# A written table of step orders, one-pass cumulative sums and a folded query norm in a two-block transformer kernel

## The chip, the cores and the metric

The kernel runs on one core of a Trainium2 chip. The metric is the device time of one execution in microseconds. A core has five engines that run their own queues in order: TensorE (PE, with its weight loads shown as PEld), VectorE (DVE), ScalarE (ACT), GpSimd (POOL) and SyncE (SP), which here issues all DMAs. They wait for one another through semaphores.

## What is computed

The reference is one layer of two different transformer blocks, over 512 positions of width 1024, in fp32. The parts around the change are the first block's two causal attentions and the second block's delta rule, which is followed by a norm over each head:

```python
def stick_breaking_attention(q, k, v):          # 8 heads of 64
    ...
    log_rem = jnp.where(strict, jax.nn.log_sigmoid(-z), 0.0)
    after = lax.cumsum(log_rem, axis=3, reverse=True) - log_rem
    w = jnp.where(strict, jnp.exp(jax.nn.log_sigmoid(z) + after), 0.0)
...
def _gated_deltanet(q, k, v, alpha, beta, a_log, dt_bias):   # 8 heads of 128, chunks of 64
    q = _l2norm(_to_chunks(q.astype(f32), A_HEADS, A_DK)) * (A_DK ** -0.5)
    k = _l2norm(_to_chunks(k.astype(f32), A_HEADS, A_DK))
    ...
    U = ut - jnp.einsum("bhck,bhkv->bhcv", wt, S)
    o = jnp.einsum("bhck,bhkv->bhcv", qt, S) + jnp.einsum("bhcj,bhjv->bhcv", pt, U)
    ...
oa = rmsnorm_2(oa, head_norm[l]) * jax.nn.silu(za.reshape(b, s, A_HEADS, A_DV))
```

Here `_l2norm(x)` is `x * rsqrt(sum(x * x) + EPS)` and `rmsnorm_2` divides by the root of the mean square plus `EPS`, 1e-6. Beside these there are a forgetting attention (8 heads of 64), a memory attention, gates, a banded attention with bias (16 heads of 64), a cross attention (4 heads of 256) and two feed-forward parts.

## The kernel before

All weight products (`Schedule.gemm`, `product`) multiply a 128x128 weight block with 512 columns of the transposed activations. Both operands are split into a high and a low part in fp32r, and three matmuls replace one (high by high, high by low, low by high: L1065, L1067, L1071). SyncE loads four blocks (`stage`), ScalarE makes their high parts (`whi`, L1520), VectorE or GpSimd the low parts (`wlo`, L1917, L2411). A step `mm` is two blocks, so six matmuls; a gemm over 1024 inputs is four such steps and an eviction step `ev`. Everything else on TensorE is an fp32 matmul through the helper `mm` (L1017) or a transpose (L1020).

`Schedule` builds one list of steps, and each engine goes through this list in the same order and issues what is its own. A part of the kernel is a generator that yields steps; an empty step keeps a distance. `mix` and `pipe` take turns between generators, and `par` spreads several lists evenly over one another by their lengths:

```python
        i = min((i for i in range(len(parts)) if done[i] < len(parts[i])), key=lambda i: (done[i] + 0.5) / len(parts[i]))
        yield parts[i][done[i]]
```

The parts that `par` spreads are, with names used below:
- `sb_pair(p)`, four pairs of stick-breaking heads, beside the weight products of the next pair: scores (`sb_z`), absolute value, exponential and logarithm (`sb_ln`), softplus (`sb_sp`), the cumulative sum on TensorE (`sb_cum`, in five pieces between which VectorE adds later blocks to earlier ones, `sb_after`), weights (`sb_w`), values (`sb_o`).
- `soft_pair("fox", p, ...)` beside products with head norms (`hn_sq`, `hn_mm`, `hn_out`) and `mem_pair(n)`, whose scaled softmax (`mp_n`, tile `sbW`) TensorE transposes.
- for each head h of the delta rule: products of head h+1 with its convolutions, silu and l2 norms (`gdn_proj`), preparation (`gdn_prep`: `gp_kk`, `gp_xy`, then five times `gp_P` and `gp_Y`, `gp_uw`) and the scan of head h-1 (`gdn_scan`: `gc_w` and `gc_s` for eight chunks, called W and S with the chunk's number below, `gc_o`, the output norm, `gs_oz`). A `gc_s` needs VectorE's subtraction into `cuu` after `gc_w`.
- band attention, the memory norm and the cross attention, each beside weight products.

A "spare" bank is the one of the two gemm banks that the running gemm does not use. A norm's ones-product goes there, and the next gemm can open only when ScalarE's logarithm has read it.

Of the kernel before, what the change touches and what calls it, by code (L numbers as in the profile page):

```python
# [8 lines left out]
F32 = mybir.dt.float32  # L9
# [7 lines left out]
T = 512  # L17
# [26 lines left out]

IDLE = 20
# [96 lines left out]
class Kernel:  # L142
# [43 lines left out]
    def allocate(self):  # L186
        sb, two = self.sb, range(2)
        self.x, self.eps = sb("x", [128, 8, T]), sb("eps", [128, 1])
# [27 lines left out]
    def allocate_block1(self):  # L216
# [14 lines left out]
        self.sbA, self.sbW = [sb(f"sbA{i}", [128, 1280]) for i in two], [sb(f"sbW{i}", [128, 1280]) for i in two]  # L231
# [15 lines left out]
    def allocate_block2(self):  # L247
# [5 lines left out]
        self.ce = [sb(f"ce{i}", [128, T]) for i in two]  # L253
# [69 lines left out]
def par(*parts):  # L323
    parts = [list(p) for p in parts]
    done = [0] * len(parts)
    while any(n < len(p) for n, p in zip(done, parts)):
        i = min((i for i in range(len(parts)) if done[i] < len(parts[i])), key=lambda i: (done[i] + 0.5) / len(parts[i]))
        yield parts[i][done[i]]
        done[i] += 1


@dataclass(eq=False)
class Norm:
# [14 lines left out]
    u_out: Use  # L348
    halves: tuple = ()
# [24 lines left out]
class Schedule:  # L374
# [3 lines left out]

# [29 lines left out]
    def halved_norm(self, no, out, u_out, raw, raw_ref, ones, scale, gain):  # L408
# [3 lines left out]
                 Use("sqb1", [("hn_out", no)]), Use("spare", [("hn_ln", no)]), u_out, (k.ofx[0][:, 3, :], k.ofx[1][:, 3, :]))  # L412
# [92 lines left out]
    def sb_pair(self, p):  # L505

        two = []
        for hh in range(2):
# [4 lines left out]
            u["A"], u["W"] = Use(f"sbA{hh}", [("pe_cum", (h, 0))]), Use(f"sbW{hh}", [("pe_o", h)])  # L513
# [128 lines left out]
    def block1(self):  # L642
# [5 lines left out]
        nxt = [mix(self.left, pipe(self.sb_proj(1)), islice(norm, 9)), mix(pipe(self.sb_proj(2) + kv[0]), norm), pipe(self.sb_proj(3) + kv[1]), seq(  # L648
            self.proj("w_in", 3072, k.qr[0][:], Use("qr0", [("pe_small", "fox")]), "mix"),
            mix(self.fox_forget(None), pipe(self.fox_proj(0))))]  # L650
# [5 lines left out]
        yield [st("none", None, *(Use(f"mq{i}", ends[i // 2]) for i in range(4)), *(Use(f"mmp{x}", ends[x]) for x in range(2)),  # L656
                  *(Use(f"{n}{x}", [("pe_cum", (("sb", 3, x), 0))]) for n in ("fxp", "fxpt", "mmpt") for x in range(2)))]
# [64 lines left out]
    def gdn_proj(self, h):  # L722
# [11 lines left out]
        if h == 8:  # L734
            yield [x for s_ in later(7) for x in s_]
            for _ in range(5):
                yield []
# [1923 lines left out]
```

## Time and profile before

| | |
|---|---|
| median of 3 runs | 2276.83 us (2276.15 to 2276.99) |
| profiled execution, its own time | 2276.96 us |
| its span, first to last instruction | 2274.9 us |
| instructions | 34567 |
| TensorE busy | 2238.1 us, 98% |
| VectorE busy | 1192.0 us, 52% |
| ScalarE busy | 932.0 us, 41% |
| GpSimd busy | 424.9 us, 19% |
| granted TensorE clock | 0.999 of full speed |

All of it is from one execution. Matmuls are pipelined and their ends are modelled, so the start of one matmul to the start of the next says more than the busy time. The stages in the trace: start to 28 us, stick-breaking pairs to 190, forgetting and memory pairs to 360, gates and first feed-forward to 930, start of the delta rule to 985, its heads to 1345, gates and band attention to 1790, cross attention to 1870, second feed-forward to the end.

### The profile page before, as it was taken

The numbers are of one execution on the slowest core, as the hardware profiler recorded it, in microseconds if no ns is written. First come the engines' busy times: TensorE is split into PE (matmuls) and PEld (weight loads), VectorE is DVE, ScalarE is ACT, GpSimd is POOL, SyncE is SP. The second block draws the span as 40 slices with busy tenths as digits, with TensorE's granted clock in tenths as the row PEclk, the third lists the DMA queues.
The fourth block names the chain that finished last, engine by engine and source line by source line (L and its number), as shares of the span: only waits on it lengthen the run. The fifth ranks groups of instructions, "written<-read, shape, count | busy, mean of one in ns | idle before, by whom it ended". The sixth has DMA issues, their size and how long they took to land.

```text
span 2274.9 us, 34567 instructions
## 1 busy us (share of the span) xinstructions
PE 2238.1 (98%) x13120; PEld 1796.2 (79%) x13120; DVE 1192.0 (52%) x2236; ACT 932.0 (41%) x1761; POOL 424.9 (19%) x356
## 2 busy tenths in 40 slices
PE   9999999999999999999999999999999999999998
PEld 6776778888888888777777788777788988888887
DVE  5435654445644546565556514665656446535454
ACT  5544554333322323444444332444435534323234
POOL 2332221001201102423343242000011001101001
PEclk9999999999999999999999999999999999999999
DMA  5223212333333333321121124223233413332332
GB/s 176 82 62 96 70 49 77 97 98 98 96 96 96 97 97 93 101 78 52 52 60 59 43 70 129 80 84 84 66 93 108 142 49 102 93 102 93 102 93 93
DMA packets 108643, 199.60 MB, mean 88 GB/s; under 512 B 12208, under 2 KB 14384, under 8 KB 108224
## 3 DMA queue, kind: packets, MB, share of 16 engines
q1 hardware_dynamic: 108480, 197.41, 28.7%
q8 instruction: 105, 1.72, 0.3%
q14 instruction: 58, 0.48, 0.1%
HBM read 195.20 MB, written 2.16 MB: 87 GB/s over the span
## 4 chain that ended last, share of the span: by engine, by line
PE 94%; DVE 3%; ACT 2%; issue 1%; DMA 0%; SPq 0%; POOL 0%; DVEq 0%; ACTq 0%
PE bank L1065 26%; PE bank L1071 25%; PE bank L1067 25%; PE bank L1017 14%; PE bank L1020 3%; DVE ya L1917 0%; DVE sbA L2107 0%; DMA x<-in_xT 0%; DVE fout L1917 0%; DVE sqb L1917 0%; ACT sbA L1661 0%; DVE acc L1917 0%; ACT sqb L1560 0%; DVE cx L1920 0%; ACT hh L1539 0%
## 5 line engine op out<-in xcount | busy, mean ns | idle before, releaser
L1065 PE MATMUL bank<-hh,whi 128*128 128x512 f32 x1680 | 684.2, 407 | 4.8 <-ACT sqb L1560 2.5
L1071 PE MATMUL bank<-hh,wlo 128*128 128x512 f32 x1680 | 656.7, 391 | 1.2 <-POOL wlo L2411 0.6
L1067 PE MATMUL bank<-hl,whi 128*128 128x512 f32 x1680 | 655.2, 390 | 0.3 <-DVE hl L1920 0.3
L1520 ACT ACTIVATE whi<-stage 128x512 fp32r<-128x512 f32 x682 | 425.4, 626 | 551.0 <-PE bank L1071 542.2
L1917 DVE TENSOR_TENSOR wlo<-stage,whi 128x512 fp32r<-128x512 f32 x506 | 408.3, 825 | 88.6 <-ACT whi L1520 84.6
L1065 PEld LDWEIGHTS bank<-hh,whi 128*128 128x128 f32 x1680 | 315.8, 188 | 75.3 <-issue 5.3
L1071 PEld LDWEIGHTS bank<-hh,wlo 128*128 128x128 f32 x1680 | 315.3, 188 | 70.7 <-DVE wlo L1917 1.9
L1067 PEld LDWEIGHTS bank<-hl,whi 128*128 128x128 f32 x1680 | 316.2, 188 | 63.2 <-issue 3.8
L2411 POOL TENSOR_TENSOR wlo<-stage,whi 128x512 fp32r<-128x512 f32 x176 | 234.2, 1336 | 450.9 <-ACT whi L1520 450.8
L1917 DVE TENSOR_TENSOR x<-bank,x 128x512 f32<-128x512 f32 (+1 forms) x81 | 55.5, 685 | 176.0 <-PE bank L1071 175.9
L1065 PE MATMUL bank<-u1h,whi 128*128 128x512 f32 x256 | 99.6, 389 | 0.0
L1067 PE MATMUL bank<-u1l,whi 128*128 128x512 f32 x256 | 99.6, 389 | 0.0
L1071 PE MATMUL bank<-u1h,wlo 128*128 128x512 f32 x256 | 99.6, 389 | 0.0
L2411 POOL TENSOR_TENSOR acc<-acc,sqb 128x512 f32<-128x512 f32 x34 | 45.7, 1345 | 283.1 <-ACT sqb L1533 283.1
L2411 POOL TENSOR_TENSOR u1l<-f1t,u1h 128x512 fp32r<-128x512 f32 x32 | 41.3, 1292 | 264.4 <-ACT u1h L1632 264.4
L2411 POOL TENSOR_TENSOR u2l<-f2s,u2h 128x512 fp32r<-128x512 f32 x22 | 28.4, 1290 | 299.0 <-ACT u2h L1641 299.0
L1017 PEld LDWEIGHTS bank<-ya 64*64 64x64 f32 (+1 forms) x2048 | 58.5, 137 | 25.0 <-issue 14.7
L1017 PE MATMUL bank<-ya 64*64 64x64 f32 (+2 forms) x2048 | 72.0, 231 | 1.9 <-DVE ya L1917 1.9
L1065 PE MATMUL bank<-u2h,whi 128*128 128x512 f32 (+1 forms) x182 | 69.7, 383 | 0.0
L1067 PE MATMUL bank<-u2l,whi 128*128 128x512 f32 (+1 forms) x182 | 69.6, 383 | 0.0
L1071 PE MATMUL bank<-u2h,wlo 128*128 128x512 f32 (+1 forms) x182 | 69.5, 382 | 0.0
L1632 ACT ACTIVATE u1h<-f1t 128x512 fp32r<-128x512 f32 x32 | 20.3, 634 | 111.4 <-DVE f1t L1917 111.4
(377 smaller groups left out, 3376.1 us busy)
## 6 DMA issues: line engine op xcount, KB each, us to landing
stage<-in_wall SPq DMA_DIRECT2D x682, 256.0 KB, 2.7
band<-in_toep SPq DMA_DIRECT2D x16, 256.0 KB, 3.5
x<-in_xT SPq DMA_DIRECT2D x8, 256.0 KB, 6.0
fb<-rowsf SPq DMA_DIRECT2D x8, 256.0 KB, 3.9
gbc<-rows SPq DMA_DIRECT2D x8, 256.0 KB, 3.3
gbc<-rowsc SPq DMA_DIRECT2D x16, 128.0 KB, 3.6
out_y<-fout SPq DMA_DIRECT2D x8, 256.0 KB, 2.5
memx<-in_memT SPq DMA_DIRECT2D x1, 1024.0 KB, 9.5
```

What stands on the lines that cost most here:

```text
L1017: return pe.matmul(out, w, r, start=start, stop=stop, skip_group_check=True)
L1020: return pe.transpose(out, in_, k.cf("ident"))
L1065: pe.matmul(o, wh, hi, start=j == 0, stop=False)
L1067: pe.matmul(o, wh, lo, start=False, stop=False)
L1071: i = pe.matmul(o, wl, hi, start=False, stop=end)
L1520: act.activation(k.whi[u % NSPLIT][:], k.stage[u % NSTAGE][:], ACT.Copy).then_inc(*up("whi", u))
L1632: act.activation(k.u1[0][:, a["t"] % 16, :], a["b"][:], ACT.Copy).then_inc(*up("sp_hi", ("u1", a["t"])))
L1917: return dve.tensor_tensor(out, a, b, op)
L2411: return pool.tensor_tensor(out, a, b, op)
```

## The change

Three things change together.

`par` and the empty steps go. `paced(key, work, *chains)` takes the same steps without the empty ones, as strands: letter a is all weight products in a row, the next letters are the tails of products that have one (turn or head norm), and the last letters are the chains (pair, preparation, scan). It yields them in the order that the string `ORDERS[key]` spells. There are 26 strings.

The cumulative sum of a stick-breaking head is made in one go. ScalarE copies the softplus tile into fp32r (`sb_high`, into the space of `ofx`), VectorE subtracts to get the low part (`sb_low`, in the space of `sbW`), and TensorE adds all blocks with two fp32r passes of ten matmuls each. The constants `ntri` and `nones` are copied once into fp32r (`cfr`). The five pieces and VectorE's additions between them go.

The query of the delta rule is no longer normalized. ScalarE squares it with a factor (`query_square`), GpSimd adds that to the square of the output (`scan_sum`), and the output norm uses another epsilon (`eps2`), so that the norm of the output makes up for the query's. `gp_qd` and the query-key product wait for the silu instead of the norm. The third buffer set `gq2` takes the place of `ce`.

```diff
+ORDERS = {
+    "sb0": "eadeaadadaeadaeadaedaaedcaaedaedab",
+    "sb1": "haggaagaagaaaghaagaaahggagaahaaaabcaaacahahdcaaadadahaaaeaheeafff",
...
+    "sb3": "aafaafabafabafaaafcaacfcaaadaafafdaed",
...
+    "fox0": "gaagagaaabgaagbabgaacgaacgagcaagdaadgadgaaegaaeagaefg",
...
+    "fox3": "bacacabcacbaacacbbcaabaccabacabcacaabccbaacabacbacacbcabcabac",
...
+    "head0": "caaacacabcababbabacacabbbbbbaaccacbacbbabbcaacabacb",
...
+    "head": "acdcacdcaadabbbbcbadaacdcdacacabbbbcdabcdacbdbcabcadcbacbdacbacdabcadbc",
...
+    "band": "caaccacaacacacacaacacbcacacacac",
...
+    "cross3": "bcabcacbabcbcbcabccbacba",
+}
...
-        self.sbA, self.sbW = [sb(f"sbA{i}", [128, 1280]) for i in two], [sb(f"sbW{i}", [128, 1280]) for i in two]
+        self.sbA = [sb(f"sbA{i}", [128, 1280]) for i in two]
+        self.cfr = sb("cfr", [128, 256], F32R)
+        m4 = len(self.open)
+        self.sbl = [sb(f"sbl{i}", [128, 1280], F32R) for i in two]
+        self.close(m4)
+        self.sbW = [sb(f"sbW{i}", [128, 1280]) for i in two]
+        self.sbh = [flat(o)[:, 0:1280] for o in self.ofx]
...
-def par(*parts):
-    parts = [list(p) for p in parts]
-    done = [0] * len(parts)
-    while any(n < len(p) for n, p in zip(done, parts)):
-        i = min((i for i in range(len(parts)) if done[i] < len(parts[i])), key=lambda i: (done[i] + 0.5) / len(parts[i]))
-        yield parts[i][done[i]]
-        done[i] += 1
-
...
+    def paced(self, key, work, *chains):
+
+        strands, tails, needs = [[]], {}, {}
+        for n, (g, tail, *need) in enumerate(work):
+            for x in need:
+                needs.setdefault(x, len(strands[0]))
+            strands[0] += [s for s in g if s]
+            if tail:
+                tails[len(strands)] = n
+                strands.append([s for s in tail if s])
+        strands += [[s for s in c if s] for c in chains]
+        order = ORDERS[key]
+        left = [iter([s for s in c if s[0][0] not in ("need", "mark")]) for c in strands]
+        for c in order:
+            yield next(left[ord(c) - 97])
+        assert not any(next(c, None) for c in left), key
...
-            u["A"], u["W"] = Use(f"sbA{hh}", [("pe_cum", (h, 0))]), Use(f"sbW{hh}", [("pe_o", h)])
+            u["A"], u["W"] = Use(f"sbA{hh}", [("sb_hi", h), ("sb_lo", h)]), Use(f"sbW{hh}", [("pe_o", h)])
+            u["H"], u["L"] = Use(f"sbh{hh}", [("pe_cum", h)]), Use(f"sbW{hh}", [("pe_cum", h)])
             two.append(Head(h, "sb", p, hh, u, "osb"))
         yield [st("sb_z", two, *(o.uses[b] for o in two for b in range(3)))]
         yield [st("sb_ln", o, o.uses["A"]) for o in two]
         yield []
         yield []
-        yield [st("sb_sp", o) for o in two]
-        a, b = two
-        yield [st("sb_cum", (a, 3))]
-        for s in (2, 1, 0):
-            yield [st("sb_cum", (a, s)), st("sb_cum", (b, s + 1))]
-        yield [st("sb_cum", (b, 0)), st("sb_w", a, a.uses["W"])]
-        yield [st("sb_w", b, b.uses["W"])]
+        yield [st("sb_sp", o, o.uses["H"], o.uses["L"]) for o in two]
+        yield [st("sb_low", o) for o in two]
+        yield []
+        yield [st("sb_cum", o) for o in two]
+        yield [st("sb_w", o, o.uses["W"]) for o in two]
         yield []
         yield [st("sb_o", two, *(o.uses["o"] for o in two))]
         yield [st("out", o) for o in two]
...
-            yield from par(self.sb_pair(p), nxt[p])
+            pair = self.sb_pair(p)
+            if p == 0:
+                yield from self.paced("sb0", self.sb_proj(1), self.left, head, pair)
+            elif p == 1:
+                yield from self.paced("sb1", self.sb_proj(2) + [(g, n, "mem") for g, n in kv[0]], rest + [[st("mark", "mem")]], pair)
+            elif p == 2:
+                yield from self.paced("sb2", self.sb_proj(3) + kv[1], pair)
+            else:
+                first = (self.proj("w_in", 3072, k.qr[0][:], Use("qr0", [("pe_small", "fox")]), "mix"), self.fox_forget(None))
+                yield from self.paced("sb3", [first] + self.fox_proj(0), pair)
         ends = [[("pe_o", ("sb", 3, x))] for x in range(2)]
         yield [st("none", None, *(Use(f"mq{i}", ends[i // 2]) for i in range(4)), *(Use(f"mmp{x}", ends[x]) for x in range(2)),
...
+            u = Use(f"gq2{h % 3}", [("oq", h)])
             yield from unit("k", 1.0)
+            yield [st("q2", (h, u), u)]
             yield from conv("v")
-            yield from unit("q", 128 ** -0.5)
-        yield from mix(products(), chain())
...
-        yield from self.norm(("oa", h), o, None, o, ("gc_o", h), k.cf("ones"), 1 / 128, k.vec("head_norm_2"),
-                             bank="b6", work=(k.gcell[c]["u"][:], k.gcell[c]["wt"][:], f"cu{c}", f"cwt{c}"))
+        o, no = k.goT, ("oa", h)
+        n = Norm(no, o, o, k.cf("ones"), 1 / 128, k.vec("head_norm_2"), T, ("gc_o", h), k.gcell[c]["u"][:], k.gcell[c]["wt"][:],
+                 Use(f"cu{c}", [("pe_hn", no)]), Use(f"cwt{c}", [("hn_out", no)]), Use("b6", [("hn_ln", no)]), None,
+                 ("oq", h), k.eps2[:, 0:1])
+        yield [st("hn_sq", (n, None), n.u_sq), st("oq", (h, n.sq))]
+        yield []
+        yield []
+        yield [st("hn_mm", n, n.u_bank, n.u_r)]
+        yield [st("hn_out", n)]
+        yield [st("need", ("silu", h))]
...
-            yield from par(*g)
+                work = work + list(pre_gates(h - 7))
+            yield from self.paced(f"head{h}" if h in (0, 1, 6, 7, 8) else "head", work, *chains)
         yield from self.gated("a2", "mix2", [("w_in_2", 7184)], [("w_a_out_2", "oa", 8)], k.a2buf, pre, True)
...
-        pe.wait_ge(*at("hn_sq", o.no))
+        pe.wait_ge(*at(*(o.summed or ("hn_sq", o.no))))
...
-    def sb_cum(o, s):
-        n, reg, A = T - 128 * s, sb_regions(o), k.sbA[o.hh]
-        wait(("sb_sp", o.no))
-        i = mm(reg[s], k.cf("ntri"), A[:, woff[s]:woff[s] + n], False, s == 3)
-        if s < 3:
-            if s < 2:
-                pe.wait_ge(*at("sb_after", (o.no, s + 1)))
-            i = mm(reg[s][:, 128:], k.cf("nones"), A[:, woff[s + 1]:woff[s + 1] + n - 128], False, True)
-        i.then_inc(*up("pe_cum", (o.no, s)))
+    def sb_cum(o):
+        reg = sb_regions(o)
+        ntri, nones = k.cfr[:, 0:128], k.cfr[:, 128:256]
+        wait(("cfr", 0))
+        for part, ref in ((k.sbh[o.hh], "sb_hi"), (k.sbl[o.hh][:], "sb_lo")):
+            pe.wait_ge(*at(ref, o.no))
+            for s in (3, 2, 1, 0):
+                i = mm(reg[s], ntri, part[:, woff[s]:woff[s] + T - 128 * s], False, s == 3 and ref == "sb_lo")
+                for j in range(s + 1, 4):
+                    i = mm(reg[s][:, 128 * (j - s):], nones, part[:, woff[j]:woff[j] + T - 128 * j], False, j == 3 and ref == "sb_lo")
+        i.then_inc(*up("pe_cum", o.no))
...
-        wait(("hn_out", ("l2q", h)))
+        wait(("silu", ("q", h)))
...
+    def sb_high(o):
+        free(o.uses["H"])
+        act.wait_ge(*at("sb_sp", o.no))
+        act.activation(k.sbh[o.hh], k.sbA[o.hh][:], ACT.Copy).then_inc(*up("sb_hi", o.no))
+
     def sb_weights(o):
         W = k.sbW[o.hh]
         free(o.uses["W"])
-        act.wait_ge(*at("pe_cum", (o.no, 0)))
...
+    def query_square(h, use):
+        free(use)
+        wait(("silu", ("q", h)))
+        act.activation(k.q2[h % 3][:], k.g3[h % 2]["q"][:], ACT.Square, scale=128 * EPS ** 0.5).then_inc(*up("gq2", h))
...
+            act.wait_ge(*at("ld_cg", 0))
+            act.activation(k.cfr[:, 0:128], k.cf("ntri"), ACT.Copy).then_inc(*up("cfr", 0))
+            act.activation(k.cfr[:, 128:256], k.cf("nones"), ACT.Copy).then_inc(*up("cfr", 0))
...
-    def sb_after(o, s):
-        if 0 < s < 3:
-            n, A = T - 128 * s, k.sbA[o.hh]
-            c = A[:, woff[s] + 128:woff[s] + n]
-            dve.wait_ge(*at("pe_cum", (o.no, s)))
-            tt(c, c, A[:, woff[s + 1]:woff[s + 1] + n - 128], ALU.add).then_inc(*up("sb_after", (o.no, s)))
+    def sb_low(o):
+        free(o.uses["L"])
+        dve.wait_ge(*at("sb_hi", o.no))
+        tt(k.sbl[o.hh][:], k.sbA[o.hh][:], k.sbh[o.hh].bitcast(F32), ALU.subtract).then_inc(*up("sb_lo", o.no))
...
+    def scan_sum(h, sq):
+        wait(("gq2", h))
+        pool.wait_ge(*at("hn_sq", ("oa", h)))
+        tt(sq, sq, k.q2[h % 3][:], ALU.add).then_inc(*up("oq", h))
```

## Rows read from the trace of the kernel before

**Rows 1.** Busy time by stage: stretch, length, engines with instruction counts, clock, DMA.

```profile
28.00:190.00 162.00, 156.81 (x838) 119.05 (x838) 65.88 (x116) 81.07 (x145) 59.67 (x50) 1.00 0.27 79
190.00:360.00 170.00, 162.65 (x926) 122.64 (x925) 99.57 (x264) 91.65 (x231) 46.81 (x35) 1.00 0.21 61
360.00:930.00 570.00, 570.00 (x2512) 471.35 (x2512) 294.45 (x395) 188.40 (x311) 74.14 (x57) 1.00 0.32 96
930.00:985.00 55.00, 51.69 (x436) 39.70 (x434) 35.75 (x61) 27.37 (x47) 21.00 (x18) 1.00 0.33 103
985.00:1345.00 360.00, 351.26 (x3662) 273.90 (x3663) 192.51 (x420) 149.97 (x239) 128.57 (x106) 1.00 0.19 55
1345.00:1790.00 445.00, 445.00 (x2392) 352.19 (x2391) 245.43 (x573) 202.90 (x443) 46.86 (x50) 1.00 0.33 98
1790.00:1870.00 80.00, 78.47 (x486) 69.74 (x485) 36.70 (x97) 33.40 (x89) 0.00 (x0) 1.00 0.23 70
```

**Rows 2.** TensorE's waits: waited for, us in total, times, longest us.

```profile
PE bank L1017 <- DVE cuu L1917: 5.6, 11, 0.6
PE bank L1020 <- DVE sbW L2122: 3.9, 5, 1.6
...
PE bank L1065 <- ACT sqb L1560: 2.5, 3, 0.8
...
PE bank L1067 <- DVE o3l L1917: 0.2, 1, 0.2
```

**Rows 3.** Timeline of TensorE in one head: start, us, line, out<-in.

```profile
1061.76 0.33 PE L1017 MATMUL bank<-cqd,cs 128*128 128x64 f32 x2
1061.90 0.48 PE L1065 MATMUL bank<-hh,whi 128*128 128x512 f32 x1
...
1065.11 0.33 PE L1017 MATMUL bank<-cqd,cs 128*128 128x64 f32 x2
1066.04 0.46 PE L1017 MATMUL bank<-cuu,ckd 128*128 128x128 f32 x2 [0.60 <-DVE cuu L1917]
```

**Rows 4.** Chain that ended last, in pair 2's cumulative sum: start, us, what.

```profile
129.34 0.12 PE bank L1065
...
130.05 0.88 PE bank L1017 x6
...
132.36 1.73 PE bank L1017 x8
...
135.74 2.58 PE bank L1017 x8
...
139.75 1.51 PE bank L1017 x4
```

**Rows 5.** Groups by line and shape, 0 to 200 us: busy, mean ns, idle before.

```profile
L1920 DVE SCALAR_TENSOR_TENSOR sbA<-bank,sbA 128x512 f32<-128x512 f32 x16 | 10.2, 680 | 2.0 <-ACT sbA L1663 2.0
...
L1920 DVE SCALAR_TENSOR_TENSOR nm1tmp<-memx,vecs,nm1r 128x256 f32<-128x256 f32 x8 | 6.0, 756 | 0.2
...
L1920 DVE SCALAR_TENSOR_TENSOR sbA<-bank,sbA 128x256 f32<-128x256 f32 x8 | 3.3, 412 | 0.0
...
L1661 ACT ACTIVATE sbA<-sbA 128x1280 f32<-128x1280 f32 x8 | 10.1, 1262 | 11.0 <-DVE sbA L1923 11.0
```

**Rows 6.** The same groups, 985 to 1345 us.

```profile
L1920 DVE SCALAR_TENSOR_TENSOR gq<-cx,vecs,gq 128x512 f32<-128x512 f32 x18 | 13.4, 747 | 0.2
...
L2411 POOL TENSOR_TENSOR wlo<-stage,whi 128x512 fp32r<-128x512 f32 x64 | 88.0, 1382 | 178.1 <-ACT whi L1520 177.9
...
L1520 ACT ACTIVATE whi<-stage 128x512 fp32r<-128x512 f32 x64 | 40.1, 627 | 146.5 <-PE bank L1071 146.5
...
L1594 ACT ACTIVATE cu<-ya 128x512 f32<-128x512 f32 x7 | 4.4, 622 | 0.0
```

**Rows 7.** Timeline of TensorE at the query norm's ones-product.

```profile
1089.29 1.12 PE L1017 MATMUL bank<-sqb,cft 128*128 128x512 f32 x2
1089.85 0.79 PE L1065 MATMUL bank<-hh,whi 128*128 128x512 f32 x1
1090.48 0.39 PE L1067 MATMUL bank<-hl,whi 128*128 128x512 f32 x1
```

More of the change, by code:

```diff
@@ L252, in allocate_block2 @@
         self.cx = [sb(f"cx{i}", [128, T + 3]) for i in two]
-        self.ce = [sb(f"ce{i}", [128, T]) for i in two]
+        self.q2 = [sb(f"gq2{i}", [128, T]) for i in range(3)]
         self.g3 = [{n: sb(f"g{n}{i}", [128, T]) for n in "qkv"} for i in two]
@@ L647, in block1 @@
         norm = self.mem_norm(1, "g_mem_norm")
-        nxt = [mix(self.left, pipe(self.sb_proj(1)), islice(norm, 9)), mix(pipe(self.sb_proj(2) + kv[0]), norm), pipe(self.sb_proj(3) + kv[1]), seq(
-            self.proj("w_in", 3072, k.qr[0][:], Use("qr0", [("pe_small", "fox")]), "mix"),
-            mix(self.fox_forget(None), pipe(self.fox_proj(0))))]
+        head, rest = list(islice(norm, 9)), list(norm)
         for p in range(4):
@@ L672, in pre_gates @@
                 pre[m, j] = b[:], place
[L673 to L676 removed]
+                yield self.proj("w_in", gcol[j] + 128 * m, b[:], Use(place, []), "mix"), None
+        back = [[mem_proj(0) + mem_proj(1) + self.fox_proj(1)],
+                [mem_proj(2) + self.fox_proj(2), blocks(0, 2)],
+                [mem_proj(3) + self.fox_proj(3), blocks(2, 5)],
                 [pre_gates(), blocks(5, 8)]]
@@ L682, in block1 @@
                     yield [st("fox_rows", (h, u), u)]
-            yield from par(self.soft_pair("fox", p, "fx", "ofx"), *back[p])
+            yield from self.paced(f"fox{p}", back[p][0], self.soft_pair("fox", p, "fx", "ofx"), *back[p][1:])
         yield [st("fence", "mg1"), st("lo_engine", "dve")]
@@ L734, in gdn_proj @@
         if h == 8:
[L735 to L749 removed]
+            return [], later(7)
+        work = []
+        for n in "kqv":
+            j, x = "qkv".index(n), CX[n]
+            work.append((self.proj("w_in_2", 128 * (8 * j + h), k.cx[x][:, 3:3 + T], Use(f"cx{x}", [("conv", (n, h))]), "mix2"), None))
+        work.append((self.proj("w_in_2", 3072 + 128 * h, k.gz[h % 3][:], Use(f"gz{h % 3}", [("gs_oz", h)]), "mix2"), None))
+        freed = {"q": [("pe_qk", h), ("gp_qd", h), ("gq2", h)], "k": [("pe_ktr", h)], "v": [("pe_vtr", h)]}
         def conv(n):
[L752 to L753 removed]
+            yield [st("need", ("w_in_2", 128 * (8 * "qkv".index(n) + h), 0))]
             u = Use(f"g{n}{s}", freed[n])
@@ L829, in block2 @@
         yield from self.proj("w_in_2", 4096, k.goT, Use("goT", [("pe_small", "gdn")]), "mix2")
-        yield from mix(self.gdn_scalars(), self.gdn_proj(0))
+        work, chain = self.gdn_proj(0)
+        yield from self.paced("gdn", work, self.gdn_scalars(), chain)
         pre = {}
@@ L1442, in tensor_program @@
         elif kind == "sb_cum":
-            sb_cum(*a)
+            sb_cum(a)
         elif kind == "sb_o":
@@ L1849, in scalar_program @@
             sb_log(a)
+        elif kind == "sb_sp":
+            sb_high(a)
         elif kind == "sb_w":
@@ L1883, in scalar_program @@
             sigmoids(*a)
+        elif kind == "q2":
+            query_square(*a)
         elif kind == "gp_eg":
@@ L2242, in prep_qd @@
         free(u["qd"])
[L2243 removed]
+        wait(("silu", ("q", h)))
         tt(C["qd"][:], q[:], k.gRk, ALU.mult).then_inc(*up("gp_qd", h))
@@ L2333, in vector_program @@
             sb_softplus(a)
-        elif kind == "sb_cum":
-            sb_after(*a)
+        elif kind == "sb_low":
+            sb_low(a)
         elif kind == "out":
@@ L2484, in pool_program @@
             decay(*a)
+        elif kind == "oq":
+            scan_sum(*a)
         elif kind == "gs_oz":
```

81 lines of the change are left out of this document (42 added, 39 removed).

## The prediction

> **What bounds the kernel now.** The table by stage comes first. In 360 to 930 us 2512 matmuls fill 570.00 us, one every 0.227 us, while VectorE is busy for 294 and ScalarE for 188 of them [rows 1]. A matmul's end is modelled, so a full TensorE alone would prove little, but a steady 0.227 us for 512 columns does: here and in the band attention (1345 to 1790, 445.00 of 445.00) TensorE has no idle time at all. A gain must come from TensorE work that is taken out or from TensorE's waits. The same table says where they are: 5.19 us in the stick-breaking pairs (162.00 less 156.81), 7.35 in the forgetting and memory pairs, 3.31 in the start of the delta rule, 8.74 in its heads, 1.53 in the cross attention, 26.1 in all [rows 1]. The list of TensorE's waits (24 rows, 54 waits; its first and last row are shown) names the scan's subtraction `cuu`, the scaling of the memory softmax `sbW` and the logarithm of a norm [rows 2]. Last, the timeline shows what a wait costs. The product that reads `cqd` is followed after 0.14 us by the next instruction where nothing is missing (1061.76 to 1061.90), and after 0.93 us where `cuu` is (1065.11 to 1066.04) [rows 3]: 0.79 us lost, of which the row calls 0.60 idle. So the modelled tail hides 0.19 us, and all waits cost up to 26.1 + 54 x 0.19 = 36 us. The table of orders can give back no more, since it removes no step.
>
> **Part 1, the cumulative sums (`sb_cum`).** Before, a pair of heads has five pieces: the chain shows 0.88, 1.73, 2.58 and 1.51 us [rows 4], and the first (128 columns, a quarter of the 512 in the 0.88 piece) adds 0.22: 6.92 us a pair, 27.7 for four. That is fp32 at 1.72 ns a column. After, each head runs two parts (high, low) of ten fp32r products: one of 512 columns, two of 384, three of 256, four of 128. In fp32r 512 columns take 0.227 us [rows 1] and 256 take 0.12 [rows 4], so 384 take about 0.175. A 128-column fp32r product is not in the trace. Its bounds: the columns' share of 0.227 plus the fixed 0.013 that the two widths leave (0.067), or no cheaper than 256 columns (0.12). A part is then 0.227 + 0.35 + 0.36 + 4x = 1.20 to 1.42 us, a pair (four parts) 4.8 to 5.7, the saving 4.9 to 8.5 us in all. I take x in the middle, at 0.09, so 6.9, less a little for the second wait inside the block: **6.5 us**. It all lies on TensorE and counts in full.
>
> The Trainium skill (TensorE: Matmul & The Clock Gate, Back-to-back issue gap) gives about 81 ns for 128 columns in a stream with weight loads, which would make a part 1.26 us. The same sentence gives 131 ns for 512 columns, where the trace disagrees with 0.227 us; no run here shows the first figure yet.
>
> Elsewhere it costs, per head, one ScalarE copy of 1280 columns, as long as the exponential of that width, 1.26 us, and one VectorE subtraction of 1280 columns: 1.77 us by the softplus rows (0.68 + 0.68 + 0.41), up to 3.1 with one GpSimd split of 1.38 in its way. Two small additions go [rows 5, 6]. These lie between scores and sum. Head a's chain is today absolute value 1.77, exponential and logarithm 2.5, softplus 1.77: 6.1 us. After, its high copy stands behind head b's exponential and logarithm (1.77 + 5.06 + 1.26 = 8.1) and its low part is there at 9.8. Cover: in `sb0` eight product steps (a step is two blocks, six matmuls, 1.36 us) stand between scores and sum, 10.9 us; in `sb3` seven, 9.5 us, and two forget-gate steps; in `sb1` and `sb2` twelve or more. So the longer chain is just covered in pairs 0 and 3. What is queued behind it on ScalarE are weight splits (`whi`), which TensorE needs; without the cover it costs 3 to 4 us in each of two pairs. The copy of the constants waits on ScalarE for the second load of constants, which VectorE waits for at the same step today while TensorE goes on; nothing.
>
> **Part 2, the folded query norm.** Its ones-product goes. From its start to the second weight product behind it are 1.19 us [rows 7]; without it one spacing, 0.23, so 0.96 us a head, or 0.88 by columns (512 x 1.72 ns). I take 0.9: **7.2 us** over eight heads, all on TensorE. ScalarE loses a square, a logarithm and an exponential and gets one square, VectorE loses a multiplication; neither sets the end. GpSimd gets one addition of 512 columns a head, about 1.4 us by its split of that width [rows 6], inside the chain of the output norm, with weight splits queued behind it. In the steady table (`head`) scan end, copy, square, addition and ones-product are spread over three product steps and a preparation product, 4.7 us, against 0.6 + 0.6 + 1.4 us of work [rows 6] and a split (0.6 on ScalarE, 1.4 on GpSimd) in the way, 4.6 us. Covered, barely; without it, about 1 us a head.
>
> **Part 3, the orders.** I read each string as the steps it spells and looked for dependent steps with no product step between, and for ones-products right before a gemm that needs their bank.
> - Forgetting and memory pairs: the memory scaling and the norms make 6.4 of today's 7.35 us [rows 1, 2]. In `fox0` to `fox3` the scaling nearly always has a product step or a score block before its transpose, and each ones-product has a product step behind it before the next gemm opens. Gain 6, range 2 to 9.
> - Stick-breaking pairs: 5.19 us today, and the longer chain takes some back. Gain 2, range -3 to 6.
> - Start of the delta rule: gain 1.5 of 3.31 (`head0` still has the third `gp_P` directly before `gp_Y`).
> - Heads: 8.74 us. `head` separates all scan steps but `W4` and `S4`, so one wait as in rows 3 stays in each head. Gain 4, range 0 to 8.
> - Cross attention: gain 0.5 of 1.53. Band, feed-forwards: no wait today, nothing to gain; two product steps still stand before each last softmax block.
> The hidden tails of some 20 waits that go, 3.8 us, half offset by new ones, give 2 more: **16 us**, between 0 and 30 (36 less `W4` `S4` in eight heads).
>
> Sum: 6.5 + 7.2 + 16 = 29.7 us. The profiled span of 2274.9 goes to 2245.2; its execution took 2276.96, the median of the runs is 2276.83, so I predict **2247 us**.
>
> **Rivals.**
> *The table gives nothing net* (13.7 us, so 2263). The arithmetic lands, but new waits in the longer stick-breaking chain and at the thin places of `head` equal those removed. For it: the even spread leaves only 26 us idle, and two covers above are thin. Against: the waits in the fox pairs are of a kind that one product step cures. Chance 0.25.
> *The table gives nearly everything* (13.7 + 30, so 2233). For it: nearly every wait is under 1 us and one step is 1.36. Against: engines work in order and the strings put several steps of one engine in a row. Chance 0.12.
> *The one-pass sums are no cheaper*, that is, the change does not do what it says: if narrow fp32r products cost what the fp32 ones do, 6.5 us are lost, 2253.5. For it: no row at 128 columns; against it: 0.12 us at 256. Chance 0.07.
> *Slower.* In `head` four convolution steps of the query stand directly before the scan's `W5`. VectorE works in order, so the subtraction that `S5` waits for is queued behind them, up to 4 x 0.75 us [rows 6], and an eviction of 0.68 [rows 5]. Cover: two product steps and the preparation products between, 3.8 us. If each two-input operation met one of GpSimd's (the memory norm's operation of 256 columns takes 0.76 where the softplus one takes 0.41 [rows 5]), the block would grow by up to 4 us. It decides from 2.3 us more in each of eight heads: 18.4 against 13.7, at 2281.5. Against it: nothing of this size appears now, and GpSimd is busy for 129 of 360 us [rows 1]. Chance 0.05.
> The Trainium skill (GPSIMD Engine Reference, Key points) says that GpSimd shares its SBUF interfaces with VectorE and contends with two-input operations; by that rule, with which the trace agrees (0.76 against 0.41 us), this rival is possible.
>
> **How the numbers follow.** The forecast (2240 to 2257) has 0.48; 0.03 is left for a time within 0.2% (4.6 us, about what a measurement of this kernel can tell from no change). The range 2236 to 2264 leaves out most of the rival with nearly everything, the slower one and the unchanged time, about 0.2. Faster 0.91, same 0.04, slower 0.05.
>
> **What would show each step.** After: each cumulative sum one stretch of some 2.6 us a head; one ones-product fewer in each head; idle TensorE time in the forgetting pairs under 3 us; heads 1.4 us shorter each; no idle in the band. Wrong would be: a wait for `sbh` or `sbl` above 1 us a pair, a wait for the GpSimd addition at the output norm, or waits for `cuu` of more than 1 us a head.

## The result, and the profile after

The changed kernel takes 2237.9 us (median of 4 runs, 2237.2 to 2240.8) against 2276.9 before: a ratio of 0.983 [0.982, 0.985], 39 us less where the forecast had 29.7. Its profiled execution has a span of 2235.4 us (2274.9 before).

The table by stage (stretch, length, busy TensorE with its matmuls, granted clock, DMA share, GB/s), cut at the first product of each stage (the granted clock is the share of full speed that TensorE was given):

```profile
28.09:185.09 157.00, 149.93 (x883) 1.00 0.27 81
185.09:345.79 160.70, 160.70 (x928) 1.00 0.22 65
345.79:916.20 570.41, 570.41 (x2514) 1.00 0.32 97
916.20:941.08 24.88, 24.88 (x127) 1.00 0.26 74
941.08:1315.90 374.82, 370.62 (x3983) 1.00 0.21 64
```

TensorE still bounds every stage. What is left to see in length minus busy time is 7.1, 0, 0, 0 and 4.2 us. Between the same products before it was 5.1, 7.4, 0, 1.2 and 10.8: it is gone in the forgetting pairs and in the start of the delta rule and fell in the heads, but it rose in the stick-breaking pairs. Between the same products of both traces the stages changed as follows (us; sb from the first scores to the first scores of fox, heads from the first `kk` product to the first weight product on `oa`):

| stage | before | after | difference |
|---|---|---|---|
| stick-breaking pairs (sb) | 162.8 | 157.0 | -5.8 |
| forgetting and memory pairs (fox) | 169.4 | 160.7 | -8.7 |
| start of the delta rule | 28.5 | 24.9 | -3.6 |
| its heads | 393.1 | 374.8 | -18.3 |
| weight products behind the heads | 67.5 | 65.9 | -1.6 |
| band attention | 215.8 | 215.9 | 0.1 |
| memory of the cross attention, cross attention | 235.4 | 233.8 | -1.7 |
| everything else | | | 0 |

The list of TensorE's waits has 12 rows instead of 24 [rows 2]; these lead it, and the scan's `cuu` is the sixth:

```profile
PE bank L1067 <- ACT sqb L1646: 2.0, 1, 2.0
PE bank L1067 <- ACT cwt L1856: 1.8, 2, 0.9
...
PE bank L1067 <- DVE cuu L1986: 1.2, 4, 0.3
```

The memory scaling, 3.9 us in five waits, is gone, and so are all waits of 990 to 1195 us but the four for `cuu` between `W4` and `S4`, which the prediction had read out of the string. They show 0.3 instead of 0.6 us idle [rows 3].

### The profile page after: what moved, and what is told of

It is laid out like the page before. It is cut to its first block, busy times and chain, and to the rows that moved or that the text cites. A ratio compares the mean times of both kernels' runs of the same rounds, so it can differ in the third digit from the quotient of the medians.

```text
span 2235.4 us, 34603 instructions
## 1 busy us (share of the span) xinstructions
PE 2213.3 (99%) x13152; PEld 1800.3 (81%) x13152; DVE 1203.6 (54%) x2221; ACT 935.1 (42%) x1755; POOL 436.3 (20%) x364
## 4 chain that ended last, share of the span: by engine, by line
PE 97%; DVE 1%; ACT 1%; issue 0%; DMA 0%; SPq 0%; DVEq 0%; ACTq 0%
PE bank L1115 27%; PE bank L1121 26%; PE bank L1117 26%; PE bank L1067 15%; PE bank L1070 3%; DMA x<-in_xT 0%; DVE fout L1986 0%; DVE acc L1986 0%; DVE sbA L1992 0%; DVE ya L1986 0%; ACT hh L1591 0%; ACT sbA L1715 0%; SPq L2579 0%; ACT sbA L1713 0%; DVE oml L1986 0%
## 5 line engine op out<-in xcount | busy, mean ns | idle before, releaser
L2477 POOL TENSOR_TENSOR wlo<-stage,whi 128x512 fp32r<-128x512 f32 x176 | 241.3, 1378 | 373.2 <-ACT whi L1572 373.0
```

The lines of the kernel that those rows point to most:

```text
L2477: return pool.tensor_tensor(out, a, b, op)
```

## The experiments

All are compared with the kernel before, on the same chip and beside it. Times of two experiments that are set against each other can come from different chips; the kernel before differs by about 0.5 us between these. "Even" is the even spread of before in place of the table.

### e1_sums: part 1 alone

The kernel before with the new `sb_pair`, `sb_cum`, `sb_high` and `sb_low`, and nothing else of the diff.

> The kernel before with part 1 alone: one-pass cumulative sums in fp32r, everything else, the even spread included, as before. In the trace of the changed kernel the chain of a pair's sum took 5.53 us instead of 6.92, four times: if that is all that part 1 gives, this kernel takes 2276.9 - 5.6 = 2271.3 us (2270.5 to 2272). The forecast's term was 6.5 (2270.4). Rival: the visible idle of the sb stage (about 6 us in both kernels) is moved by the extra wait for the high and low halves, and part 1 costs more beside work than it gives: 2274 to 2277.

Measured: 2283.0 us, 1.0027 [1.0017, 1.0036]. Part 1 alone makes the kernel **slower by 6.0 us**, though a pair's sum took 5.5 us here as well. My theory for it is wrong, and by more than the rival said. The stage went from 162.8 to 167.4 us and its idle time from 5.1 to 13.4. In the list of waits of the whole kernel (waited for, us in total, times, longest) the row for `v` has grown from 1.1 us in one wait, and that for `lf` is new:

```profile
PE bank L1070 <- ACT v L1613: 7.8, 3, 3.4
...
PE bank L1022 <- DVE lf L1937: 2.7, 1, 2.7
```

ScalarE's timeline at the longest of them shows the queue (start, us, line, out<-in, idle before):

```profile
77.69 1.14 ACT L1527 ACTIVATE whi<-stage 128x512 fp32r<-128x512 f32 x2
81.78 1.27 ACT L1675 ACTIVATE ofx<-sbA 128x1280 fp32r<-128x1280 f32 x1 [2.94 <-DVE sbA L1937]
83.30 1.27 ACT L1675 ACTIVATE ofx<-sbA 128x1280 fp32r<-128x1280 f32 x1 [0.25 <-DVE sbA L1937]
84.48 1.13 ACT L1527 ACTIVATE whi<-stage 128x512 fp32r<-128x512 f32 x2
85.52 0.57 ACT L1613 ACTIVATE v<-bank 128x512 f32<-128x512 f32 x1
```

TensorE had turned `v` by 81.8. Its bank comes free only with the copy at 85.52, because ScalarE first waited 2.94 us for VectorE's softplus and then made both copies to the high half. TensorE stood for 3.43 us.

That wait has a second price. The table by microseconds of the same place (length, busy TensorE, granted clock, DMA):

```profile
84.00:85.00 1.00, 0.00 (x0) 1.00 0.00 0
85.00:86.00 1.00, 0.00 (x0) 1.00 0.00 0
86.00:87.00 1.00, 0.85 (x7) 1.00 0.00 0
87.00:88.00 1.00, 1.00 (x8) 0.61 0.00 0
88.00:89.00 1.00, 1.00 (x7) 0.50 0.34 111
...
90.00:91.00 1.00, 1.00 (x7) 0.68 0.78 180
91.00:92.00 1.00, 1.00 (x10) 1.00 0.69 213
```

A good microsecond after TensorE is busy again its granted clock is 0.50, the lower of its two levels (1.2 GHz), until 90.6. That loses 0.39 + 0.50 + 0.50 + 0.32 = 1.7 us. There is one such stretch behind this wait and one at the end of that for `lf`: 3.4 us. For the stage that makes -5.6 for the sums, +8.3 idle and +3.4 clock, 6.1 us, where it grew by 4.6; the other 1.5 are not explained. The profiled execution as a whole is 5.7 us longer (2280.6 against 2274.9): the stage, 0.5 us ahead of it, and 0.7 in a wait for `bv` behind the heads that before did not have.

### e2_even: parts 1 and 2, no table

> The changed kernel with all 26 orders replaced by the even spread of before: parts 1 and 2 alone. Theory T (the table makes about 26 of the 39 us): 2276.9 - 5.6 - 7.7 = 2263.6 us (2262 to 2265). Rival N (with the query norm gone the head's chains are shorter, and most of what the heads gained beyond the arithmetic comes without the table): heads then give 18 us here, and the kernel takes 2250 to 2254 us. The forecast's own sum of parts 1 and 2 was 13.7: 2263.2.

Measured: 2284.6 us, 1.0033 [1.0020, 1.0047]. Both theories fail. Part 2 alone costs another 1.6 us where its eight products should have given 7. The heads take 396.7 us (before 393.1), and the leading wait was one of 0.3 us before:

```profile
PE bank L1125 <- DVE cs L2047: 12.0, 16, 1.1
```

The stick-breaking stage has the same products in the same order as in e1_sums and yet took 1.2 us more (168.6): the stretch at the lower clock behind the wait for `v` is twice as long in this execution. So a difference of 1 to 2 us between two of these kernels can be the clock's.

Parts 1 and 2 are worth nothing under the even spread, then, and the orders bring 46.7 us on top of them, not 26. e3, e4 and e10 say where, e5, e6 and e9 why.

### e3_heads, e4_fox, e10_sb: the table in one stage

> As e2_even, but the orders of the table in the head periods (head0 to head8) and only there. Theory T: the table in the heads gives what the stage lengths show beyond the query norm, 18.3 - 7.7 = 10.6 us below e2_even, so about 2253 us. By the forecast's term (4 us for the heads, of visible waits) it would be 4 us below e2_even, about 2259.5. Rival N: 0 to 3 us below e2_even, which would itself be near 2252.

Measured: 2264.4 us, 0.994 [0.993, 0.996]: **20.2 us** below e2_even, twice what I expected.

> As e2_even, but the orders of the table in the fox pairs (fox0 to fox3) and only there. Theory T: 7.2 us below e2_even (the stage went from 159.6 to 152.4 us), about 2256.4 us; by the forecast's term, 6 us below. Rival: the stage's gain is in part that of its neighbours (the order of sb3, which hands over to it), and fox alone gives 3 us or less below e2_even.

Measured: 2275.7 us, 0.9992 [0.9983, 1.0002]: **8.9 us** below e2_even. The stage took 160.7 us, as in the changed kernel; the order of the pairs ahead of it has no part in that.

> As e2_even, but the orders of the table in the sb pairs (sb0 to sb3) and only there. The stage took 168.6 us in e2_even and 157.0 us in the changed kernel, so 11.6 us below e2_even: 2273.0 us. Theory: of the 11.6 us some 7 are the waits themselves and some 4 the granted clock, which fell to 0.83 and 0.91 in two stretches of 20 us behind waits of about 3 us in e2_even, and has no such stretch in the sb stage of the changed kernel; so the clock stays at 1.00 here. Rival: the falls have nothing to do with the waits, and come here as well (2276 to 2277).

Measured: 2275.3 us, 0.9995 [0.9985, 1.0004]: **9.3 us** below e2_even, where I expected 11.6. The stage's idle time fell from 13.4 to 6.2 us, and what the clock takes in it from 5.1 to 1.7. Its profiled execution still shows one stretch at 0.50, behind a wait of 1.0 us at 153, a wait that the changed kernel has too, without such a stretch. The clock's fall needs no long wait, then, and does not follow each short one.

The three give 38.4 of the 46.7 us. By the stage lengths the rest is 1.9 in the start of the delta rule, 1.6 in the first head, which begins right behind it (39.9 us in e3_heads, 38.2 in the changed kernel), 1.3 behind the heads, 1.7 in the cross attention, and the 1.7 that the clock still takes in e10_sb. Before the end of the execution the lower clock costs e2_even's trace 5.1 us and that of the changed kernel nothing: some 5 of the 46.7 us are the clock's, by these single executions.

### e5_late_high: the copies one step later

```diff
-        elif kind == "sb_sp":
+        elif kind == "sb_low":
             sb_high(a)
```

> e1_sums with one thing moved: ScalarE issues the two copies to the high half one step later, in the step of the low half; the products and their order stay. Theory P (part 1 loses at the even spread because the copies of 1.27 us, which wait for VectorE's softplus, stand in ScalarE's queue ahead of the copy of the transposed v that frees TensorE's next bank, 7.8 us in three waits): most of that wait goes, and the kernel takes 2283.0 - 7.8 = 2275.2 us (2272 to 2277). Rival: the sum itself is late then, the wait only moves to the products of the cumulative sum, and it stays within 2 us of 2283.

Measured: 2278.1 us, 1.0006 [0.9997, 1.0016], 4.9 us below e1_sums. The wait for `v` fell from 7.8 to 3.8 us (two waits, the longest 2.4), with a new one of 0.6 for `sbl`. So the place of the two copies is shown to be what makes the wait. The profiled execution has no stretch at the lower clock in the stage, but it is the shortest of the ten (2276.5; they reach 2281.2), and eight of them have a mean granted clock of 0.997 or 0.998 instead of 0.999. How much of the 4.9 us is the clock is therefore open. One step is too little of a move for pair 1, where the copies still stand ahead of `v`, so half of the wait stays.

### e6_pad and e9_phase: why part 2 gave nothing

e6_pad is e2_even, with a chain of the projections that has as many steps as before the change:

```diff
-            yield from unit("k", 1.0)
-            yield [st("q2", (h, u), u)]
+            key = list(unit("k", 1.0))
+            key[-1] = key[-1] + [st("q2", (h, u), u)]
+            yield from key
             yield from conv("v")
+            yield from repeat([], len(key))
```

> e2_even with the number of steps that the folded query norm took from the projection's chain put back as empty steps (five at its end) and the square of q joined to the step before it, so that the even spread puts the convolutions and the scan where it put them before the change; nothing else differs. Theory P (parts 1 and 2 save their time on TensorE, but shift where the even spread puts the rest; at the shifted place the state update waits behind a convolution, 12.0 us in 16 waits): the head stage falls from 396.7 us to 393.1 - 7.7 = 385.4 us, and the kernel takes about 2273.3 us (2271 to 2276). Rival (the square on ScalarE and the addition on GpSimd lengthen the scan's norm and make the waits themselves): it stays at 2283 to 2286.

Measured: 2288.4 us, 1.0050 [1.0035, 1.0065]; the heads took 400.4 us. Theory P fails in this form: with the projection's steps put back it got worse. TensorE's timeline shows what it waits for, 10 us into a head:

```profile
1153.73 0.28 PE L1127 MATMUL bank<-cuu,ckd 128*128 128x128 f32 x1
1153.84 0.33 PE L1127 MATMUL bank<-cpt,cuu 128*128 128x64 f32 x2
1155.32 0.49 PE L1127 MATMUL bank<-cs,cwt 128*128 128x128 f32 x2 [1.14 <-DVE cs L2049]
```

`cs` is the state that `S(n)` (the products with `ckd`) updates and `W(n+1)` (those with `cs`) reads. They stand next to each other, with nothing in between to cover the update. VectorE's timeline of the same place shows a second reason. The product was done at 1154.0, but the update had to stand behind two operations of the preparation and one convolution step:

```profile
1154.54 0.47 DVE L2331 TENSOR_SCALAR gk<-cx,vecs 128x512 f32<-128x512 f32 x1
1154.93 0.33 DVE L2049 SCALAR_TENSOR_TENSOR cs<-cs,ceg,bank 128x128 f32<-128x128 f32 x1
```

The head stage has 48 such updates. The 22 whose reader follows directly all show a wait: 0.27 us where VectorE had been idle, up to 1.14 where it had not. The 26 with another product in between show none. Without that neighbourhood there is no wait, and VectorE's queue makes some 7 of the 12.9 us.

The scan, too, has one step more than before: its norm has a second empty one, so that GpSimd's sum fits in. That moves its every step. e9_phase takes out this one:

```diff
         yield [st("hn_sq", (n, None), n.u_sq), st("oq", (h, n.sq))]
         yield []
-        yield []
         yield [st("hn_mm", n, n.u_bank, n.u_r)]
```

> e6_pad with one empty step fewer in the scan, between the square of the head's output and its ones-product. With that, TensorE's program of a steady head period is that of the kernel before, product for product, without the query norm's one; in e6_pad the products of W(n+1) stood directly behind those of S(n) in four places, with no weight product between. Theory P (what parts 1 and 2 lose at the even spread is lost by where the spread puts the scan's steps, and one step more in the scan is enough): the head stage takes 393.1 - 7.7 = 385.4 us, up to 388 if the ones-product now waits for GpSimd's sum, and the kernel 2288.4 - 15.0 = 2273.4 us (2271 to 2276). Rival (the square on ScalarE and the sum on GpSimd slow VectorE or the chain, wherever the steps stand): 2282 to 2288 us.

Measured: 2274.7 us, 0.9990 [0.9980, 0.9999]: as theory P said, and **13.7 us** less than e6_pad for one empty step. The two tables of the head stage, of e6_pad and then of e9_phase (length; busy PE, PEld, DVE, ACT and POOL):

```profile
963.40:1363.80 400.40, 378.40 (x3978) 295.60 (x3978) 214.09 (x451) 157.53 (x246) 145.74 (x124) 1.00 0.19 57
```

```profile
964.00:1351.10 387.10, 376.25 (x3978) 295.02 (x3978) 219.53 (x451) 157.69 (x246) 149.21 (x124) 1.00 0.21 58
```

The same products (x3978) and the same work on the other engines; 11.1 of the 13.3 us are idle time that went. In the order of before, without the query's product, the heads take 387.1 instead of 393.1 us and the start of the delta rule 26.7 instead of 28.5: part 2 is worth 7.8 us. The rival, that square and sum do harm by themselves, is out.

The same trace shows why the idle time understates what an order costs. The first two rows stand 0.45 us apart, with no idle time named. Where nothing is late, as in the changed kernel below, a small product starts 0.24 us behind a weight product (1129.16 to 1129.40):

```profile
1157.07 0.40 PE L1180 MATMUL bank<-hh,wlo 128*128 128x512 f32 x1
1157.52 0.46 PE L1126 MATMUL bank<-cuu,ckd 128*128 128x128 f32 x2
...
1159.03 0.33 PE L1126 MATMUL bank<-cqd,cs 128*128 128x64 f32 x2
1159.95 0.46 PE L1126 MATMUL bank<-cuu,ckd 128*128 128x128 f32 x2 [0.59 <-DVE cuu L2045]
```

```profile
1129.16 0.39 PE L1121 MATMUL bank<-hh,wlo 128*128 128x512 f32 x1
1129.40 0.38 PE L1067 MATMUL bank<-cs,cwt 128*128 128x128 f32 x2
1129.62 0.33 PE L1067 MATMUL bank<-cqd,cs 128*128 128x64 f32 x2
1130.24 0.46 PE L1067 MATMUL bank<-cuu,ckd 128*128 128x128 f32 x2 [0.29 <-DVE cuu L1986]
```

A lateness of 0.21 us hides wholly in the modelled end of the product ahead. Not every longer distance is lateness, though. In e9_phase's trace a product of 64 rows starts 0.32 us behind a weight product, and in the heads before, in e9_phase and in the changed kernel such a start has a median of 0.326 us, against 0.230 for a product of 128 rows:

```profile
1154.03 0.40 PE L1180 MATMUL bank<-hh,wlo 128*128 128x512 f32 x1
1154.35 0.68 PE L1126 MATMUL bank<-ya 64*64 64x64 f32 x16
```

### e7_group: what a narrow product costs

```diff
             for s in (3, 2, 1, 0):
-                i = mm(reg[s], ntri, ...)
-                for j in range(s + 1, 4):
+                mm(reg[s], ntri, ...)
+            for s in (2, 1, 0):
+                for j in range(s + 1, 4):
                     i = mm(reg[s][:, 128 * (j - s):], nones, ...)
```

> The changed kernel with the products of the cumulative sum grouped within each part: first the four of the triangle, then the six of the ones, instead of in turns. The same products, sizes and waits. Theory A (a product of 128 columns costs about 0.115 us because loading its 128 weights bounds it): no change, 2237.9 us, and a pair's sum stays at 5.53 us. Theory B (changing from one set of weights to the other costs about 0.057 us each time, three changes back and forth in each of four parts): a pair's sum falls by about 0.7 us, and the kernel to about 2235.2 us.

Measured: 2239.4 us (2237.9 to 2240.9), 0.983 [0.982, 0.985]: no change. The timeline of a pair's sum, of the changed kernel and then of e7_group:

```profile
41.87 1.51 PE L1067 MATMUL bank<-ofx,cfr 128*128 128x128 f32 x10
43.21 1.56 PE L1067 MATMUL bank<-sbl,cfr 128*128 128x128 f32 x10
44.61 1.56 PE L1067 MATMUL bank<-ofx,cfr 128*128 128x128 f32 x10
46.00 1.55 PE L1067 MATMUL bank<-sbl,cfr 128*128 128x128 f32 x10
47.40 0.45 PE L1115 MATMUL bank<-hh,whi 128*128 128x512 f32 x1
```

```profile
42.64 1.49 PE L1067 MATMUL bank<-ofx,cfr 128*128 128x128 f32 x10
...
48.10 0.45 PE L1115 MATMUL bank<-hh,whi 128*128 128x512 f32 x1
```

5.53 us in turns, 5.46 grouped. The changes between the two sets of weights cost next to nothing, so theory B is out. The weight loads show that a part has ten of them in both kernels, one for each product, also where the weights stay the same:

```profile
43.15 1.47 PEld L1067 LDWEIGHTS bank<-sbl,cfr 128*128 128x128 f32 x10
```

```profile
43.91 1.45 PEld L1067 LDWEIGHTS bank<-sbl,cfr 128*128 128x128 f32 x10
```

So the experiment did not change the number of loads. Theory A, that loading the weights bounds a narrow product, fits these rows; it is what is left, not shown by itself.

### e8_double: a product more in each head

```diff
+        if o.no[0] == "l2k":
+            mm(bank[o.u_bank.bank][:, 0:o.n], o.ones, o.sq, True, True)
         mm(bank[o.u_bank.bank][:, 0:o.n], o.ones, o.sq, True, True).then_inc(*up("pe_hn", o.no))
```

> The changed kernel with the product of the key's norm made twice in each of the eight heads: eight products more of the form that part 2 takes away (128x512 fp32, 0.88 us by the rows before the change), in the orders of the table. Theory: TensorE bounds these periods, so all of it shows: 2237.9 + 7.0 = 2244.9 us, and part 2 is worth its full 7 to 7.7 us once the orders are right. Rival (the periods are bound by the chain of the scan, and a product beside it is hidden): 2238 to 2241 us.

Measured: 2245.3 us, 0.986 [0.984, 0.988]: 7.3 us for eight products. (The four executions took 2245.1 to 2250.5 us; the longest is the profiled one, in which the lower clock takes 5.1 us before the end.) In the table's order TensorE has no slack in the heads, and nothing hides a product of 0.88 us.

### e11_better and e12_better2: what the table leaves

e11_better moves six steps across the borders of pairs or behind a product (the ends of three strings, the first scores of fox and the two small products of the forget gates):

```diff
-    "fox0": "gaagagaaab...
+    "fox0": "aghagagaaab...
```

> The changed kernel with six steps moved that its table leaves in front of a wait: the turns of v at the ends of the first and the last sb pair, and the last norm of the second, go into the next pair, behind its first weight product (waits of 0.83, 0.81 and 1.98 us in the trace of the changed kernel); the first scores of fox stand behind a product (0.87 us); the two small products of the forget gates stand one product later (1.03 us). Theory (a wait that has a weight product put in its place is gone, with nothing late behind it): 5.5 us of waits and their tails, 2237.9 - 5.5 = 2232.4 us (2231 to 2234). Rival: the waits move to the steps behind the moved ones, 2236 to 2238.

Measured: 2236.1 us (2235.9 to 2236.6), 0.982 [0.980, 0.984]: 1.8 us less than the changed kernel, where 5.5 were to be had. The rival is right. The waits in its trace that the changed kernel did not have:

```profile
PE bank L1127 <- ACT fr L1813: 1.4, 1, 1.4
PE bank L1079 <- DVE osb L1998: 1.4, 2, 1.2
...
PE bank L1127 <- ACT sqb L1624: 0.8, 1, 0.8
```

> e11_better with three of its places changed by what its trace shows: the small products of the forget gates back where the table has them (moved, they waited 0.49 us and made the next bank wait 1.43 us, where the table's order waits 1.03); in the third sb pair the first weight product ahead of the scores, which waited 1.23 us for the second pair's output; and the seventh head in the order of the heads before it, whose first scan step stands behind a weight product (its own order starts with a wait of 0.91 us). Theory: 0.9 + 1.2 + 0.9 = 3.0 us less than e11_better, 2233.1 us (2232 to 2235). Rival, as with e11_better: half or more of it comes back as a wait of the next step, 2234.6 to 2236.

Measured: 2236.3 us (2233.9 to 2237.6, five runs), 0.982 [0.981, 0.983]. Its median is that of e11_better. Of the expected 3.0 us the idle time shows 2.2, and the profiled execution, the longest of the five, gives it back in two stretches at the lower clock. One of them:

```profile
151.00:152.00 1.00, 0.20 (x2) 1.00 0.00 0
152.00:153.00 1.00, 1.00 (x9) 1.00 0.00 0
153.00:154.00 1.00, 1.00 (x4) 0.73 0.00 0
154.00:155.00 1.00, 1.00 (x4) 0.50 0.00 0
155.00:156.00 1.00, 1.00 (x4) 0.50 0.00 0
156.00:157.00 1.00, 1.00 (x4) 0.57 0.00 0
```

It costs 1.7 us and stands behind a wait of 1.03. Two of them taken from 2237.6 leave 2234.2, near the shortest run. Both versions lie a little below the changed kernel's 2237.9; the intervals of all three overlap, so whether either is faster stays open. Two attempts at the waits that the table leaves brought less than 2 us; that no order can give more is not shown.

## Why the prediction was right, and where its sum was off

The forecast named the right mechanism and too small a size. 2237.9 lies below the 2240 to 2257 that had nearly half the chance, and inside the range of 2236 to 2264 by 2 us only. Of the 9.3 us that the sum lacked, part 3 makes 9.6, while the errors of parts 1 and 2 (-0.9 and +0.6) nearly cancel, which is luck. None of the signs of being wrong appeared: no wait for `sbh` or `sbl`, none for GpSimd's addition, `cuu` at 0.3 us. The heads became 2.3 us shorter each, not 1.4.

**The bound** was right: the change acted only through products taken out and waits of TensorE; e8_double shows it for the heads, where an added product counts in full.

**Part 1**, forecast 6.5: 4 x (6.92 - 5.53) = 5.6 us on TensorE. A part takes 1.38 us, so a 128-column product costs (1.38 - 0.227 - 0.35 - 0.36) / 4 = 0.11 us, near the upper bound of 0.12 instead of the 0.09 taken. The Trainium skill's 81 ns for this width (TensorE: Matmul & The Clock Gate, Back-to-back issue gap) does not hold for these fp32r products, by the 0.11 us here. The longer chain was rightly seen as covered in the table. What I did not see is that the copies stand ahead of `v` where there is no table; there, the step costs more than it gives.

**Part 2**, forecast 7.2: 7.8 us by e9_phase, 7.3 for the same products by e8_double. GpSimd's sum was covered, as forecast: no wait for it in the list.

**Part 3**, forecast 16 (0 to 30): the term that was mis-sized. Against the order of before, with the arithmetic taken off, the table gave 39 - 5.6 - 7.8 = 25.6 us. By stage, forecast and measured: fox 6 and 8.7; sb 2 and 0.2; start of the delta rule 1.5 and 1.8 (3.6 less the 1.8 of the first norm); **heads 4 and 12.3** (387.1 in e9_phase to 374.8); cross attention 0.5 and 1.7; behind the heads 0 and 1.6; and 2 for tails, which the stages contain. (These add up to 26.3; the profiled executions differ by 0.5 us more than the medians.) In the stick-breaking pairs the table removed no idle time, which rose by 2 us; against e2_even it undid what part 1 does there.

Two things failed, in the heads above all. From 8.7 us of idle time (10.8 between the same products) I took half; 6.7 of e9_phase's 10.9 went. And 5.6 us more went that are no idle time, where the sum had 2 for the whole kernel, because I priced hidden time at 0.19 us for each *listed* wait. Part of the 5.6 is lateness below the modelled end of a product, which no list names: starts at 0.45 us like the one above come seven times in e9_phase's heads and once in the changed kernel's, some 1.3 us. Part is the neighbours: the changed kernel has 39 products of 64 rows directly behind a weight product, e9_phase 52, again some 1.3 us. How the rest divides is not shown. The bound of 36 us left both out and was too low in its principle, though the time stayed inside it.

**The rivals.** *Nothing net from the table* (2263) is refuted, and so is its premise that the arithmetic lands by itself: e2_even has the arithmetic without the table and takes 2284.6. *Nearly everything* (2233) came closest, with 25.6 of its 30 us. *No cheaper* is refuted by the 5.53 us. *Slower*: the four convolutions before `W5` cost nothing in the table; `S5` shows no wait. Operations do grow beside GpSimd's: ten of the changed kernel's 72 three-operand convolution steps took 1.43 to 1.85 us instead of 0.75, but none of the query's, and no product waited for them. The 0.76 us that the prediction set against 0.41 was a mean of two kinds: five of the eight took 0.47 to 0.49 and two, beside a GpSimd split, 1.40 and 1.51. The rival had its mechanism half right: in e2_even and e6_pad VectorE's queue made more than half of the waits for `cs`, but only where a scan step stood directly behind the one it needs. e9_phase has all the convolutions, one step of the scan placed otherwise, and not these waits.

**The measure of the change.** Stated as one sum, parts 1 and 2 bring 13.4 and the orders 25.6 us. Stated as the steps an engineer would take, parts 1 and 2 at the even spread bring -7.7 us and the table 46.7. The prediction never asked for this second account.

## What to carry to other kernels

With in-order queues and a fixed interleaving rule, each added or removed step moves all later ones against each other: judge an arithmetic saving only after the order is fitted again, since one empty step was worth 13.7 us here and a saving of 13.4 us of TensorE work came out as a loss of 7.7. Look first for two dependent steps of one chain with no independent product between them, and for a copy that frees a bank standing behind an instruction that waits. To bound what orders can give, compare start-to-start times of the same products with the same neighbours where nothing is late, not the listed idle time alone.

## What the runs showed of the hardware

- TensorE's granted clock fell to its lower level (0.50, 1.2 GHz) for 3.4 us at a time, in three traces once for 6.8; each 3.4 us costs 1.7. Apart from the start and the end of an execution, every fall began during a wait of TensorE or within 2.4 us behind the end of one of 0.87 us or more. The length of the wait does not decide alone. The one of 3.4 us for `v` drew a fall in all six traces that have it (e1_sums, e2_even, e3_heads, e4_fox, e6_pad, e9_phase). The one of 2.9 us in the next pair drew one in e3_heads and e4_fox only. The one of 2.7 us for `lf` drew one in the same six, and none in e5_late_high. Behind the wait of 1.0 us just after 150 us it came in e7_group, e8_double, e10_sb and e12_better2, and not in the changed kernel. One profiled execution of each kernel is too little to say how often.
- An fp32r product of 128 columns costs about 0.11 us, of 256 columns 0.12, of 512 columns 0.227: below 256 columns narrowing gives almost nothing. Changing back and forth between two sets of weights adds under 0.02 us a time (0.07 us over a pair's four parts).
- A dependent product can be late by about 0.2 us without any idle time in the profile (0.45 us start to start instead of 0.24).
- The distance from a weight product to the next small one depends on its shape: 0.23 us to one of 128 rows, 0.33 to one of 64.
- A convolution step of VectorE takes 0.75 us, and 1.43 to 1.85 beside some operations of GpSimd.
